# Differential attention with natural feature order: the rotation's partner rows fetched by transfers, both maps' scores on the two halves of the matmul array

## The reference

```python
q = q.reshape(b, s, A_HEADS, 2, A_HEAD_DIM)          # A_HEADS 8, A_HEAD_DIM 64
k = k.reshape(b, s, A_HEADS, 2, A_HEAD_DIM)
q = apply_rope(q, cos, sin) * (A_HEAD_DIM ** -0.5)   # halves of 32: (x1*cos - x2*sin, x1*sin + x2*cos)
k = apply_rope(k, cos, sin)
...
sc = jnp.einsum('bqhmd,bkhmd->bhmqk', q[:, q0:kend], k[:, :kend])
p = jax.nn.softmax(jnp.where(allowed, sc, neg), axis=-1)
a = p[:, :, 0] - lam * p[:, :, 1]
outs.append(jnp.einsum('bhqk,bkhe->bqhe', a.astype(v.dtype), v[:, :kend]))
...
o = rms_norm(o, subln_g) * (1.0 - lambda_init)
```

## Time and profile before

| | |
|---|---|
| Time, median of 3 runs | 1752.66 us (1752.47 to 1754.15) |
| Profiled execution: its own time, its span | 1752.62 us, 1750.9 us |
| Busy in the span: TensorE, VectorE, ScalarE, GpSimd | 1735.2, 1204.6, 815.3, 15.1 us |
| First and last scores of the first attention (line 1069) | 68.5 and 215.2 us |
| From the S3 of one head to that of the next | 19.49 us (six times; the first turn takes 16.58) |
| Granted clock, mean | 0.999 |

### The profile page before, as it was taken

The page is one execution under the profiler, slowest core; times in us unless marked ns, Lnnn a source line. Parts: engine busy times, 40 slices in busy tenths (PEclk is TensorE's granted clock), DMA queues, the critical chain, the costliest instruction groups (busy, mean ns, idle before and its releaser), DMA issues.

```text
span 1750.9 us, 26096 instructions
## 1 busy us (share of the span) xinstructions
PE 1735.2 (99%) x10394; PEld 1501.4 (86%) x10394; DVE 1204.6 (69%) x1966; ACT 815.3 (47%) x1434; POOL 15.1 (1%) x40
## 2 busy tenths in 40 slices
PE   9999999999999999999999999999999999999998
PEld 8777779999999897666989999988888798999997
DVE  4688777877787734555877777868437786767776
ACT  4467644444444234555344444443555555333342
POOL 0000000000000000000000000000000000000001
PEclk9999999999999999999999999999999999999999
DMA  9232222433334343222233333353313224333331
GB/s 302 80 100 86 88 82 77 121 97 97 96 106 138 94 133 95 74 85 64 58 109 109 97 96 98 98 178 89 96 49 121 72 85 121 99 107 97 98 108 49
DMA packets 218219, 177.15 MB, mean 101 GB/s; under 512 B 9025, under 2 KB 177890, under 8 KB 218098
## 3 DMA queue, kind: packets, MB, share of 16 engines
q1 hardware_dynamic: 218098, 175.49, 32.7%
HBM read 173.32 MB, written 7.38 MB: 103 GB/s over the span
## 4 chain that ended last, share of the span: by engine, by line
PE 94%; DVE 4%; ACT 1%; issue 0%; DMA 0%; DVEq 0%; POOL 0%; ACTq 0%; POOLq 0%
PE ps L720 29%; PE ps L721 28%; PE ps L722 28%; PE ps L1069 2%; PE ps L1111 1%; PE ps L1135 1%; PE ps L1123 1%; PE ps L1089 1%; PE ps L965 1%; PE ps L1079 1%; DVE xl L1739 0%; PE ps L1099 0%; PE ps L950 0%; DVE wlo L1647 0%; ACT whi L1291 0%
## 5 line engine op out<-in xcount | busy, mean ns | idle before, releaser
L1647 DVE TENSOR_TENSOR wlo<-raw,whi 128x1024 fp32r<-128x1024 f32 (+1 forms) x276 | 318.0, 1168 | 193.1 <-ACT whi L1291 192.8
L720 PE MATMUL ps<-xh,whi 128*128 128x256 f32 (+1 forms) x1016 | 336.8, 331 | 2.3 <-DVE xl L1739 2.3
L722 PE MATMUL ps<-xh,wlo 128*128 128x256 f32 (+1 forms) x1016 | 325.6, 320 | 0.0
L721 PE MATMUL ps<-xl,whi 128*128 128x256 f32 (+1 forms) x1016 | 325.1, 320 | 0.0
L1291 ACT ACTIVATE whi<-raw 128x1024 fp32r<-128x1024 f32 (+1 forms) x276 | 274.6, 1007 | 82.5 <-DMA raw<-in_w_ff 36.2
L720 PE MATMUL ps<-whi,hh 128*128 128x512 f32 x728 | 290.6, 399 | 3.1 <-DVE wlo L1647 1.5
L721 PE MATMUL ps<-wlo,hh 128*128 128x512 f32 x728 | 285.2, 392 | 0.0
L722 PE MATMUL ps<-whi,hl 128*128 128x512 f32 x728 | 283.7, 390 | 0.0
L720 PEld LDWEIGHTS ps<-xh,whi 128*128 128x128 f32 x1016 | 193.4, 190 | 27.0 <-issue 10.2
L722 PEld LDWEIGHTS ps<-xh,wlo 128*128 128x128 f32 x1016 | 193.4, 190 | 14.6
L721 PEld LDWEIGHTS ps<-xl,whi 128*128 128x128 f32 x1016 | 193.6, 191 | 13.9 <-issue 1.2
(11 more groups left out here) (251 smaller groups left out, 2911.1 us busy)
## 6 DMA issues: line engine op xcount, KB each, us to landing
raw<-in_ffn_w_in SPq DMA_DIRECT2D x88, 512.0 KB, 3.9
raw<-in_w_ff SPq DMA_DIRECT2D x64, 512.0 KB, 4.1
raw<-in_ffn_w_out SPq DMA_DIRECT2D x44, 512.0 KB, 3.8
raw<-in_a_w_qkv SPq DMA_DIRECT2D x22, 512.0 KB, 4.9
raw<-in_w_in SPq DMA_DIRECT2D x20, 512.0 KB, 3.8
raw<-in_kv_w SPq DMA_DIRECT2D x16, 512.0 KB, 4.2
bias_skewed<-bias_rows SPq DMA_DIRECT2D x8, 640.0 KB
raw<-in_a_w_o SPq DMA_DIRECT2D x8, 512.0 KB, 4.3
```

What stands on the lines that cost most here:

```text
L720: e.matmul(o, ah, bh, start=start, stop=False, **more)
L721: e.matmul(o, ah, bl, start=False, stop=False, **more)
L722: return e.matmul(o, al, bh, start=False, stop=stop, **more)
L1647: e.tensor_tensor(lo[:, 0:n], src, f32(hi[:, 0:n]), ALU.subtract).then_inc(s.lo, 1)
```

## The change

Five things are done together.

1. The features stay in natural order (`halves_first` is gone): a head's 128 rows are map 0's 64, then map 1's 64. The rotation's partner of a row is 32 rows away, which DVE can't reach inside one instruction. So ACT copies the sums to the arena at `post` (`unturned`, with the factor 0.125 for q), SP issues four transfers of 32 rows (64 KB each) that bring the rows exchanged to `partner`, and a new step `rope` has DVE multiply by cosine, wait for the partner, multiply that by sine, and add.
2. Scores: each map's matmul takes 64 rows of q and k, map 0 on rows 0 to 63 and map 1 on rows 64 to 127 of the array. The second attention has that form already (line 1111 of before).
3. `masks_a` and its table are gone.
4. `ORDER_A` is new. `M` now stands for a `rope` step and comes twice in a turn; a `post` of q or k also does the rope that is outstanding, if there is one.
5. Eight of the pieces of the value projection come after q and k of head 0 instead of before.

```diff
-ORDER_A = "- t0 S3 S2 - R3 w S1 R2 - F3 - F2 M T3 n R1 - m S0 - F1 R0 l T2 F0 - - x T1 x".split()
+ORDER_A = "t0 - S3 S2 R3 - w S1 R2 - F3 M - n R1 F2 T3 - S0 m F1 R0 F0 l - - M x T2 - T1 x".split()
...
+        if job.kind in ("q_a", "k_a"):
+            self.rope()
+            self.unroped.append((job.arg, int(job.kind == "k_a")))
...
-        self.run(values)
-        self.attention_a()
+        self.some(values, 8)
+        self.attention_a(values)
...
+    def rope(self):
+
+        if self.unroped:
+            self.step("rope", *self.unroped.pop(0))
...
         self.run(proj(0))
-        self.step("masks_a", 0)
+        self.run(values)
+        self.rope()
...
                 elif name == "M":
-                    if g < 7:
-                        self.step("masks_a", g + 1)
+                    self.rope()
...
-                for m, (q, b) in enumerate(((q0, banks[0]), (q1, banks[1]))):
-                    w.wait_ge(s.halves, h + 1)
+                for b in banks:
                     w.wait_ge(s.rope, 2 * h + 2)
                     w.wait_ge(*freed[b])
-                    e.matmul(ps[b][:, 0:n], q[:, i * 128:i * 128 + 128], k[:, 0:n],
+                for m, b in enumerate(banks):
+                    c = slice(64 * m, 64 * m + 64)
+                    e.matmul(ps[b][:, 0:n], q[c, i * 128:i * 128 + 128], k[c, 0:n],
                              start=True, stop=True).then_inc(s.scores, 1)
...
+                if job.kind in ("q_a", "k_a"):
+                    u = 2 * job.arg + (job.kind == "k_a")
+                    w.wait_ge(s.job, job.n + 1)
+                    w.wait_ge(s.nlam, 1)
+                    if u >= 2:
+                        w.wait_ge(s.rope, u - 1)
+                    e.activation(self.unturned[u % 2], ps[b][:], ACT.Copy,
+                                 scale=0.125 if job.kind == "q_a" else 1.0).then_inc(s.unturned, 1)
...
-            elif what == "masks_a":
-                h, = arg
-                q0, q1, _ = self.qk_a[h % 3]
-                w.wait_ge(s.rope, 2 * h + 1)
-                w.wait_ge(s.a_in, 80)
-                e.activation(q1, q0, ACT.Copy, scale=self.masks[:, 1:2]).then_inc(s.half, 1)
-                w.wait_ge(s.half, h + 1)
-                e.activation(q0, q0, ACT.Copy, scale=self.masks[:, 0:1]).then_inc(s.halves, 1)
...
-                    e.tensor_tensor(self.tmp[0:64, :], ps[b][64:128, :], self.sinb[64:128, :],
-                                    ALU.mult).then_inc(s.dve, 1)
-                    e.tensor_tensor(self.tmp[64:128, :], ps[b][0:64, :], self.sinb[0:64, :],
-                                    ALU.mult).then_inc(s.dve, 1)
...
-                    e.tensor_tensor(dst, ps[b][:], self.cosb, ALU.mult).then_inc(s.cos, 1)
-                    w.wait_ge(s.dve, own)
-                    w.wait_ge(s.cos, u + 1)
-                    e.tensor_tensor(dst, dst, self.tmp, ALU.add).then_inc(s.rope, 1)
...
+            elif what == "rope":
+                h, which = arg
+                u = 2 * h + which
+                dst, own_half, partner = self.qk_a[h % 3][which], self.unturned[u % 2], self.partner[u % 2]
+                w.wait_ge(s.unturned, u + 1)
+                w.wait_ge(s.a_in, 64)
+                if h >= 3:
+                    w.wait_ge(s.scores, 8 * (h - 2))
+                e.tensor_tensor(dst, own_half, self.cosb, ALU.mult).then_inc(s.cos, 1)
+                w.wait_ge(s.partner[u % 2], 64 * (u // 2 + 1))
+                e.tensor_tensor(partner, partner, self.sinb, ALU.mult).then_inc(s.dve, 1)
+                own += 1
+                w.wait_ge(s.dve, own)
+                w.wait_ge(s.cos, u + 1)
+                e.tensor_tensor(dst, dst, partner, ALU.add).then_inc(s.rope, 1)
...
+            elif what == "post" and arg[0].kind in ("q_a", "k_a"):
+                u = 2 * arg[0].arg + (arg[0].kind == "k_a")
+                w.wait_ge(s.unturned, u + 1)
+                if u >= 2:
+                    w.wait_ge(s.rope, u - 1)
+                for r in range(4):
+                    to, at = r * 32, (r ^ 1) * 32
+                    e.dma_start(self.partner[u % 2][to:to + 32, :],
+                                self.unturned[u % 2][at:at + 32, :]).then_inc(s.partner[u % 2], 16)
```

More of the change, by code:

```diff
@@ L394, in network, with attention_a @@
         self.feed()
-    def attention_a(self):
+    def rope(self):
+        if self.unroped:
+            self.step("rope", *self.unroped.pop(0))
+    def attention_a(self, values):
+        self.unroped = []
         self.step("prepare_a")
@@ L757, in __init__ @@
         self.mb, self.relu, self.fb, self.fsum, self.ysq = new("mb"), new("relu"), new("fb"), new("fsum"), new("ysq")
-        self.half, self.halves, self.share0 = new("half"), new("halves"), new("share0")
+        self.unturned, self.partner, self.share0 = new("unturned"), [new(f"partner{i}") for i in range(2)], new("share0")
         self.copied, self.gates, self.x_raw = new("copied"), new("gates"), new("x_raw")
@@ L817, in __init__ @@
         self.nlam, self.g8 = small[:, 2:3], small[:, 3:4]
-        self.masks = small[:, 4:6]
         self.gocol, self.blcol = small[:, 6:10], small[:, 10:14]
@@ L829, in __init__ @@
         self.cosb, self.sinb = ar(BASE, 512), ar(BASE + 512, 512)
-        self.qk_a = [[ar(BASE + 1024 + (n * 3 + i) * 512, 512) for i in range(3)] for n in range(2)]
-        self.qk_a.append([ar(BASE + 13824 + i * 512, 512) for i in range(3)])
+        self.qk_a = [[ar(BASE + 1024 + (n * 2 + i) * 512, 512) for i in range(2)] for n in range(3)]
+        self.unturned = [ar(BASE + 13824 + i * 512, 512) for i in range(2)]
+        self.partner = [ar(at, 512) for at in (BASE + 14848, BASE + 12288)]
         self.xt = ar(BASE + 8192, 4096).rearrange("p (k c) -> p k c", k=8)
@@ L835, in __init__ @@
         self.aT = ar(BASE + 10240, 2048).rearrange("p (j q) -> p j q", j=4)
-        self.tmp, self.sq_a, self.of_a = (ar(BASE + 12288 + i * 512, 512) for i in range(3))
+        self.sq_a, self.of_a = (ar(BASE + 12800 + i * 512, 512) for i in range(2))
         self.lam4 = ar(BASE + 12288, 256)
@@ L989, in tensor @@
                     freed[b] = {
-                        "q_a": (s.cos, 2 * n - 1), "k_a": (s.cos, 2 * n), "gate": (s.silu, n), "up": (s.up, n),
+                        "q_a": (s.unturned, 2 * n - 1), "k_a": (s.unturned, 2 * n), "gate": (s.silu, n), "up": (s.up, n),
                         "q_b": (s.qk_b, 2 * n - 1), "k_b": (s.qk_b, 2 * n), "copy": (s.copy, n), "zg": (s.zg, n),
@@ L1062, in tensor @@
                 h, i, banks = arg
-                q0, q1, k = self.qk_a[h % 3]
+                q, k = self.qk_a[h % 3]
                 n = (i + 1) * 128
-                for m, (q, b) in enumerate(((q0, banks[0]), (q1, banks[1]))):
-                    w.wait_ge(s.halves, h + 1)
+                for b in banks:
                     w.wait_ge(s.rope, 2 * h + 2)
                     w.wait_ge(*freed[b])
-                    e.matmul(ps[b][:, 0:n], q[:, i * 128:i * 128 + 128], k[:, 0:n],
+                for m, b in enumerate(banks):
+                    c = slice(64 * m, 64 * m + 64)
+                    e.matmul(ps[b][:, 0:n], q[c, i * 128:i * 128 + 128], k[c, 0:n],
                              start=True, stop=True).then_inc(s.scores, 1)
@@ L1348, in scalar @@
                 b, n = job.bank, job.i
-                if job.kind == "gate":
+                if job.kind in ("q_a", "k_a"):
[6 more added lines that the diff above has]
+                                 scale=0.125 if job.kind == "q_a" else 1.0).then_inc(s.unturned, 1)
+                elif job.kind == "gate":
                     w.wait_ge(s.job, job.n + 1)
@@ L1744, in vector @@
                 b, n = job.bank, job.i
[L1745 to L1753, removed]
-                    e.tensor_tensor(self.tmp[0:64, :], ps[b][64:128, :], self.sinb[64:128, :],
-                                    ALU.mult).then_inc(s.dve, 1)
-                    e.tensor_tensor(self.tmp[64:128, :], ps[b][0:64, :], self.sinb[0:64, :],
-                                    ALU.mult).then_inc(s.dve, 1)
-                    own += 2
-                    if h >= 3:
-                        w.wait_ge(s.scores, 8 * (h - 2))
-                    e.tensor_tensor(dst, ps[b][:], self.cosb, ALU.mult).then_inc(s.cos, 1)
-                    w.wait_ge(s.dve, own)
-                    w.wait_ge(s.cos, u + 1)
-                    e.tensor_tensor(dst, dst, self.tmp, ALU.add).then_inc(s.rope, 1)
-                elif job.kind == "up":
+                if job.kind == "up":
                     f = job.arg[-1]
@@ L2216, in sync @@
                 e.dma_start(self.sinb, ap["c_sin"]).then_inc(s.a_in, 16)
-                e.dma_start(self.masks, ap["c_mask"]).then_inc(s.a_in, 16)
                 e.dma_start(self.g8, ap["a_subln_g"][0].rearrange("(p a) -> p a", a=1),
@@ L2287, in constants @@
     c = cos.T[d].astype(np.float32)
-    s = (sin.T[d] * np.where(np.arange(128) < 64, 1.0, -1.0)[:, None]).astype(np.float32)
```

(8 more changed lines are left out.)

## The result

The changed kernel takes 1779.86 us (median of 4 runs, 1779.15 to 1781.23), the kernel before 1753.33 (4 runs, 1752.47 to 1754.15): a ratio of 1.0152 [1.0135, 1.017], 26.5 us slower. The forecast was 1773 within 1757 to 1790. The profiled execution took 1779.15 us with a span of 1777.4.

A forecast was written before the change was run, and what follows sets the result against it. TensorE was taken to bound the kernel, with k's partner rows then waiting behind the copy. 1752.6 us plus 20.4 (turns 1 to 6 +18.6, turn 0 +2.6, turn 7 -0.8) gave 1773, 8 in 10 from 1757 to 1790.

The forecast's parts named there:

- The mechanism: In each turn k's partner rows queue behind the two-engine copy; DVE waits in `rope`, TensorE idles 3.9 us at S3.
- the partner passes the copy: Rival: engines alternate between the copy's packets and later ones, k's rows land in time, total 1746.5 us; chance 0.11.
- The chain: From one k rotation's end to the next: split, loads, copy 12.4 us, k's rows, sine; turn 22.6 us, +3.1.
- the forecast's margin: In the turn's chain: a little for slower-landing loads, raising the turn from 22.4 to 22.6 us.
- Turn 0: First turn of the head loop: copy issued after head 1's q transfers, 19.2 us against 16.58, +2.6.
- The clock: Rival at S3: gaps of 3.9 us may halve TensorE's clock; only the last costs, +0 to 3 us; no chance given.
- turn 7: Last turn of the head loop: it rotates nothing, so it was forecast at -0.8 us.
- The saving of TensorE: Scores on 64 rows side by side: 4.32 us a head falls to 3.56, net 0.76 a head, 6.1 for 8 heads.
- The bound of twice the speed: Rival in the scores, from the skill's tiling page: their time halves, 17 us saved, total 1735; chance 0.01.
- The cover: Between S0 and next S3: TensorE's 6.8 us of work exceeds k's rotation by 0.35; rival of too little, chance 0.05.
- Nothing for ACT, DVE, the value pieces, the start: DVE saves 11 us busy time off TensorE's path, ACT swaps masks for copies, moved value pieces cost nothing.

The follow-up runs named there:

- Experiment 1: The changed kernel with the skew copy's two outer sizes in the other order, so it uses 16 engines, same bytes: 1745.43 us, ratio 0.9956.
- 2: The changed kernel, copy still on two engines but issued in the middle of the turn, after k's partner transfers: 1750.89 us, ratio 0.9985.
- 3: The changed kernel, copy as it is, with the partner transfers issued by ACT in its own queue instead of by SP: 1757.06 us, ratio 1.0019.
- experiment 5: Experiment 1 with the scores as full-array matmuls over all 128 rows, output not the reference's: 1753.28 us, ratio 1.0002.
- experiment 6: Experiment 1 with the old order of steps, the two rotations placed in it: 1744.54 us, ratio 0.995.
- 7: Experiment 1 with all value pieces before head 0 again: 1745.26 us, ratio 0.9954.
- experiment 4: The kernel before with its copy on 16 engines: 1753.14 us, ratio 1.0001.
- experiment 8: The changed kernel with 96 of each copy's 128 rows on two engines and the last 32 as a second copy on 16: 1759.55 us, ratio 1.0035.

## Why the prediction was right, step by step

**The mechanism.** It held as forecast: first in, first out on each engine of the queue, k's rows behind the copy, DVE in `rope`, TensorE at S3. Experiment 1 removes the wait by the shape, 2 by the order in the queue and 3 by the queue. The rival "the partner passes the copy" is true only across queues. Its 1746.5, the price without any wait, was 1.1 us from experiment 1's 1745.4.

**The chain.** The forecast turn was 22.6, measured 23.34. With R the end of k's rotation, the copy started at R+7.2 by forecast. By its packets it starts at R+7.4 to R+8.3 in turns 1 to 6, on the mean R+7.7. In turn 3, R is 134.5 and the windows show the copy's beginning at 142, R+7.5:

```profile
141.00:142.00 1.00, 1.00 (x6) 0.82 (x5) 0.96 (x4) 1.00 (x4) 0.00 (x0) 1.00 0.96 373
142.00:143.00 1.00, 1.00 (x6) 0.84 (x5) 0.97 (x4) 1.00 (x5) 0.00 (x0) 1.00 0.16 58
```

The copy was costed at 12.4 and took 12.8 to 13.3 by its packets, on the mean 13.0. From its last packet to the sine product it was 1.1 to 1.7, on the mean the 1.2 of the forecast, and from there to R 1.42 instead of 1.6. The late start and the longer copy are 1.1 a turn; less the shorter last part (0.2) and the forecast's margin (0.2), 0.7 a turn was missing: +23.1 for turns 1 to 6 where +18.6 was forecast. Turn 0 was 19.26 (19.2).

**The clock.** The forecast said that gaps of this size may halve the clock, and that the slower work fits into the wait. It happened at five of the seven gaps. Two gaps of 3.0 us and those of 4.8 and 4.9 were among the five; of two gaps of 3.65 us one was and one was not, and the shortest, 1.8, was not. For the turn above, then a few microseconds behind the S3 at 158.07, then the same stretch behind one after which it did not fall:

```profile
112.00:116.00 4.00, 4.00 (x12) 2.37 (x9) 3.85 (x9) 2.02 (x6) 0.00 (x0) 0.57 0.63 177
...
158.00:162.00 4.00, 3.93 (x10) 1.73 (x11) 3.92 (x8) 0.78 (x2) 0.00 (x0) 0.50 0.36 85
...
136.00:140.00 4.00, 4.00 (x18) 2.56 (x14) 3.83 (x10) 2.21 (x7) 0.00 (x0) 1.00 0.77 200
```

0.50 is 1.2 GHz, 1.00 is 2.4. The turn at 110.82 has 20.12 us of TensorE's work where experiment 1 has 18.52, and is no longer for it, since the copy sets its end: the two turns at nearly full clock last 23.48 and 23.42, the four others after the first 22.93 to 23.77. The seven turns last 159.3 us against 126.7 in experiment 1. Of these 32.6 us the waits are 24.8 and the slower work 7.8. In turns 1 to 6 it is 4.8 a turn (3.5 idle, 1.3 slower work) where the forecast had 3.9. Its 3 us for slow work in a turn were too much: the turns hold 0.1 to 2.6. The rows it took them from do not carry them either, since for the stretch of the earlier trace rows (0 to 7 us) the windows view gives a granted clock of 1.00. Only after the last gap does slow work count. From the S3 to the S0 of turn 7 it is 14.2 us, 13.2 before and 12.6 in experiment 1: +1.0 where -0.8 was forecast, of it 1.6 slow work. What lies before the first S3 and behind the last S0 takes 0.3 us less than before.

**The saving of TensorE.** 0.76 a head by forecast, 0.97 by experiment 1 and 0.95 by experiment 5. The mis-sized part is S3 with S2: estimated at 2.11, measured 103.72 - 101.36 - 2 x 0.23 = 1.90. That two adjoining groups save 0.2 was too little; they saved 0.4. The bound of twice the speed stays rejected: 8 x 0.97 = 7.8 us and not 17.

**The cover.** 0.35 us was forecast between k's rotation and S3 (its own terms give 0.4: 0.55 + 5.85 is 6.40 and not 6.45). In experiment 1 it ends at 118.67 + 0.69 = 119.36 and S3 starts at 120.20: 0.84. The error was on the safe side, and in experiment 6 TensorE waits for no rotation even in the old order.

**Nothing for ACT, DVE, the value pieces, the start.** DVE's busy time fell from 1204.6 to 1191.6 us (11 forecast, 13 measured), ACT's from 815.3 to 814.4. Experiments 5 and 7 show that neither this nor the moved pieces change the time.

In all: the forecast was +20.4, the result +26.5. Turns 1 to 6 hold 4.5 of the difference and the last turn 1.8, less 0.3 outside the turns. So the range was hit by the mechanism that was forecast, and what separates the two numbers is several small terms.

## What to carry to other kernels

A copy's outermost size is a schedule decision. Here a size of 2 put 640 KB on two engines for 13 us, at no cost as long as nothing urgent followed in the same queue (experiment 4); before a transfer is added to a queue, list what stands ahead of it and on how many engines that runs. A DMA share of 0.13, two of 16 engines, that holds for many microseconds was the mark of this copy, and the mean of 0.26 for the turn hid it. And when a change adds a good part and a bad wait, take the wait away alone: here two lines more make a kernel of 1745.4 us, faster than both.

## What the runs showed of the hardware

- A transfer of 32 rows behind a two-engine copy was not complete before the copy's end. Of the four issued from 122.09 to 123.94, 112 of 128 packets had ended by 125.62; the last 16 started at 131.81, when the copy's last packet ended, and the wait was over at 133.1.
- Two groups of 64-row scores (512 and 384 columns) side by side in one run took 1.90 us from start to start, where the 512 alone are 1.26 and the 384 alone 1.05 by estimate, between the 1.26 and the 0.62 of 128 columns.
- Seven gaps on TensorE of 1.8 to 4.9 us: within or soon after five of them, of 3.0 to 4.9 us, the granted clock fell to 0.50; at the other two, of 1.8 and 3.65 us, it stayed at 1.00. In experiment 8, with gaps up to 2.2 us, its mean was 0.999 (0.993 in the changed kernel).
- Issuing four transfers of 64 KB took SP 2.4 to 2.7 us in 11 of the 14 cases of the changed kernel between 60 and 250 us and 3.3 in the other three; ACT took 2.8 in the case shown.
